# Layer-norm statistics kept as whole 128x512 tiles instead of columns per token

## The chip, the cores and the metric

One core of one Trainium2 chip runs the whole program. The metric is device time in microseconds, the median of several executions of the same program.

## The reference

Two layers of width 2048 over 512 tokens in fp32. Layer 0 mixes block-sparse attention and a gated linear recurrence, layer 1 is a gated causal convolution of 31 taps with a layer norm of its own. Each layer ends in a projection, a residual, a layer norm and a gated side input of 256 features. The change touches the three layer norms only:

```python
def _layernorm(x, g, b):
    mu = jnp.mean(xf, axis=-1, keepdims=True)
    var = jnp.mean(jnp.square(xf - mu), axis=-1, keepdims=True)
    return ((xf - mu) * lax.rsqrt(var + LN_EPS) * g + b).astype(x.dtype)
...
# inside layer 1:
    c = _layernorm(c, ln_g, ln_b)
    return (jax.nn.silu(c) * jax.nn.silu(z)) @ w_out
...
# after each layer:
        x = _layernorm(DEEPNORM_ALPHA * x + y, post_ln_g[i], post_ln_b[i])
        x = x + (p[i] @ ple_w[i]) * jax.nn.sigmoid(x @ ple_gate_w[i])
```

## The kernel before

The activations lie transposed, features on the 128 partitions and the 512 tokens on the free axis, as 16 chunks of 128x512 in `Y`. A weight matrix is cut into tiles of 128 outputs (128x2048, "w tile"), 177 in all. Each fp32 operand is split into a high and a low part in a format that TensorE takes in one pass, and a product is three such passes: high by high, high by low, low by high. So one w tile costs TensorE 48 matmuls of 128x512. Of a w tile ACT makes the high part (`w_hi`, L895) and DVE (L1288) or POOL (L432) the low part (`w_lo`). Of a normed chunk ACT makes the high part (`a_hi`, L899) and POOL the low part (`a_lo`, L400). Each engine's program is written out by hand in its own order, and semaphores join them. The results land in two banks, `G0` and `G1`, which must be emptied in turn.

After the last tile of a layer's output projection stands this, in `second_part`, twice in the program:

- TensorE runs two "side" w tiles, each 8 groups of 6 matmuls (`ple_pack`). Group c needs its G bank empty, and a bank is emptied by a copy on ACT (`ple_out`, L1091) or DVE (`side_out`, L1716). `SIDE_ON_ACT` and `SIDE_ON_DVE` say behind which chunk of the norm each copy stands in those engines' order.
- The norm's statistics go on beside it. `ln_sum` and `ln_sqs` hold, for each partition and token, the sum of the chunks and of their squares. TensorE sums each over the partitions into a column per 128 tokens, 128x4 in all (`to_tokens`). DVE and ACT work out mean, variance and one over the deviation on 128x4 columns: a square root on ACT, a reciprocal on DVE and one Newton step. The mean, then the reciprocal deviation, is spread over the partitions again: DVE multiplies the column into a diagonal matrix (L1673) and TensorE multiplies ones by it (`spread_mean` into `X[1]`, `spread_dev` into `X[2]`).
- DVE subtracts (L1701) and multiplies (L1705) chunk after chunk. ACT applies gain and bias (L1163) and makes `a_hi`, POOL makes `a_lo`. In the same DVE program stand the low parts of three w tiles, behind chunks 1, 7 and 9.
- TensorE then runs the first two gate tiles together (`gemm_pair`): the first takes chunk k as soon as its parts are there, the second runs 7 chunks behind. All later tiles of the gate need all 16 chunks.

The norm inside layer 1 uses the same helpers. There TensorE works on six more full w tiles of the layer meanwhile, with the two spreads inside the first of them, and the low parts of those w tiles are POOL's.

```python
            def to_tokens(bank, src):
                for m in range(NT):
                    last = mm(bank[:, m:m + 1], src[:, m * P:(m + 1) * P], ones[:, 0:1])
                return last
```

Of the kernel before, what the change touches and what calls it, by code (L numbers as in the profile page):

```python
# [101 lines left out]
def constants():  # L102
# [22 lines left out]
    half_summed=4, shift_done=1, shift_ready=1, sums_set=3, centred=16, c_summed=16, squared=16, sq_summed=16, mean_sum=1,  # L125
    var_sum=1, ln_step=6, var=1, ln_root=1, ln_guess=1, diag_d=1, diag_r=1, mean_spread=1, dev_spread=1, less_mean=16, normed=16)

# [27 lines left out]
def build(nc, xT, wall, w1, w2, pT, par_in, masks_in, out):  # L155
# [8 lines left out]
    with ExitStack() as ctx:  # L164
# [37 lines left out]
        eglast = sb("eglast", [P, NT])  # L202
        stat = bias[:, 0:5 * NT]
        lb = sb("lb", [P, 4, HEADS])
# [61 lines left out]
        ln_sq = [tmp[:, 0:T], tmp[:, T:2 * T]]  # L266
        ln_shift = diag_d = tmp[:, 2 * T:3 * T]
        ln_sqs = tmp[:, 3 * T:4 * T]
        UW = T + CONV_K - 1
        ln_sum = diag_r = tmp[:, 2 * UW + 2 * T:2 * UW + 3 * T]  # L270
        U = [tmp[:, n * UW:(n + 1) * UW] for n in range(2)]
        conv_sg = tmp[:, 2 * UW:2 * UW + T]

        c_shift = c_diag_d = tmp[:, 2 * UW + T:2 * UW + 2 * T]
        c_sq = [Z[:, 12 * T:13 * T], Z[:, 13 * T:14 * T]]
# [210 lines left out]
        def _(pe):  # L486
# [324 lines left out]
            prev_turns(HEADS)  # L811
            def to_tokens(bank, src):

                for m in range(NT):
                    last = mm(bank[:, m:m + 1], src[:, m * P:(m + 1) * P], ones[:, 0:1])
                return last

            def shift(sem, n):
# [4 lines left out]
            def token_mean(n):  # L823
                pe.wait_ge(*after("shift_ready", n, 1))
                pe.wait_ge(*after("c_summed", n, KC))
                to_tokens(X[0], ln_sum).then_inc(S("mean_sum"), 1)

            def token_var(n, sqs):
                pe.wait_ge(*after("sq_summed", n, KC))
                to_tokens(TB[2], sqs).then_inc(S("var_sum"), 1)  # L830

            def spread_mean(n, diag):

                pe.wait_ge(*after("diag_d", n, 1))
                mm(X[1][:, :], ones[:, :], diag).then_inc(S("mean_spread"), 1)

            def spread_dev(n):
                pe.wait_ge(*after("diag_r", n, 1))
                mm(X[2][:, :], ones[:, :], diag_r).then_inc(S("dev_spread"), 1)

            def second_part(layer, between=None):
                w, g = W_OUT[layer], G_OUT[layer]
                gemm_pair(w, g, f"act_hi{layer}", f"act_split{layer}", between, pair_lag=OUT_LAG[layer])
                gemms(w + 2, g + 2, 6)
                gemm(Idx(w + 8), Idx(g + 8))
                shift(*after("half_summed", 2 * layer, KC // 2))
# [7 lines left out]
                ple_pack(layer, 0, range(2, 3))
                spread_mean(n, diag_d)
                ple_pack(layer, 0, range(3, 4))
                spread_dev(n)
                ple_pack(layer, 0, range(4, 8))
# [17 lines left out]
            token_var(1, c_sqs)  # L876
            gemm(Idx(W_CONV + 42), Idx(G_CONV + 42), between={3: lambda: spread_mean(1, c_diag_d), 7: lambda: spread_dev(1)})
            gemms(W_CONV + 43, G_CONV + 43, 4)
# [8 lines left out]
        def _(act):  # L887
# [226 lines left out]
            def load_root_table():  # L1114

                f(stat[:, 3 * NT:4 * NT], ones[:, 0:NT], ACT.Sqrt)

            def deviation(n):

                var, dev = stat[:, 2 * NT:3 * NT], stat[:, 3 * NT:4 * NT]  # L1120
                act.wait_ge(*after("var", n, 1))
                f(dev, var, ACT.Sqrt).then_inc(S("ln_root"), 1)

            def second_part(layer):
# [157 lines left out]
        def _(dve):  # L1282
# [384 lines left out]

            def statistics(n, diag_of_mean):

                mean, off, var, dev, rr = [stat[:, k * NT:(k + 1) * NT] for k in range(5)]  # L1670

                def spread(dst, src):
                    return tt(dst.rearrange("p (c t) -> p c t", c=NT), ident.unsqueeze(1).broadcast_to([P, NT, P]),  # L1673
                              src.unsqueeze(2).broadcast_to([P, NT, P]), ALU.mult)

                step = S("ln_step")
                dve.wait_ge(*after("mean_sum", n, 1))
                ts(mean, X[0][:, 0:NT], 1.0 / D, None, ALU.mult).then_inc(step, 1)
                dve.wait_ge(*after("ln_step", n, 1))
                stt(off, mean, -1.0, mean, op0=ALU.mult, op1=ALU.mult).then_inc(step, 1)  # L1680
                dve.wait_ge(*after("ln_step", n, 2))
                ts(off, off, EPS, None, ALU.add).then_inc(step, 1)
                dve.wait_ge(*after("ln_step", n, 3))
                dve.wait_ge(*after("var_sum", n, 1))
                stt(var, TB[2][:, 0:NT], 1.0 / D, off, op0=ALU.mult, op1=ALU.add).then_inc(S("var"), 1)
                dve.wait_ge(*after("centred", n, KC))
                spread(diag_of_mean, mean).then_inc(S("diag_d"), 1)
                dve.wait_ge(*after("ln_root", n, 1))
                dve.reciprocal(dev, dev).then_inc(S("ln_guess"), 1)
                dve.wait_ge(*after("ln_guess", n, 1))  # L1690
                stt(rr, dev, -0.5, dev, op0=ALU.mult, op1=ALU.mult).then_inc(step, 1)
                dve.wait_ge(*after("ln_step", n, 4))
                dve.wait_ge(*after("var", n, 1))
                tt(rr, rr, var, ALU.mult).then_inc(step, 1)
                dve.wait_ge(*after("ln_step", n, 5))
                stt(dev, rr, 1.5, dev, op0=ALU.add, op1=ALU.mult).then_inc(step, 1)
                dve.wait_ge(*after("ln_step", n, 6))
                spread(diag_r, dev).then_inc(S("diag_r"), 1)

            def minus_mean(j):  # L1700
                tt(chunk(Y, j), chunk(Y, j), X[1][:, :], ALU.subtract).then_inc(S("less_mean"), 1)  # L1701

            def over_deviation(n, j):
                dve.wait_ge(*after("less_mean", n, j + 1))
                tt(chunk(Y, j), chunk(Y, j), X[2][:, :], ALU.mult).then_inc(S("normed"), 1)  # L1705

            def second_part(layer):
# [72 lines left out]
                add_last(n_ln, KC - 1, ln_sqs, ln_sq[1])  # L1780
                statistics(n_ln, diag_d)
                dve.wait_ge(*after("mean_spread", n_ln, 1))
                for j in range(3):
                    minus_mean(j)
                dve.wait_ge(*after("dev_spread", n_ln, 1))
                for j in range(KC):
                    over_deviation(n_ln, j)
                    if j + 3 < KC:
                        minus_mean(j + 3)
                    if j in (1, 7, 9):  # L1790
# [85 lines left out]
            add_last(1, KC - 1, c_sqs, c_sq[1])  # L1876
            statistics(1, c_diag_d)

# [6 lines left out]

            dve.wait_ge(*after("mean_spread", 1, 1))
            minus_mean(0)
            dve.wait_ge(*after("dev_spread", 1, 1))
            for j in range(KC + 4):
                if j + 1 < KC:  # L1890
                    minus_mean(j + 1)
                if j < KC:
                    over_deviation(1, j)
                if 4 <= j and j < KC + 2:
                    gate_c(j - 4)
# [82 lines left out]
```

## Time and profile before

| what | value |
|---|---|
| median of 3 runs | 2109.95 us (2109.76 to 2110.11) |
| profiled execution, its own time | 2109.43 us |
| profiled execution, span | 2107.8 us |
| busy: PE, PEld, DVE, ACT, POOL | 2100.7, 1743.7, 1253.4, 817.5, 365.1 us |
| granted TensorE clock over the run | 1.0 of full speed (2.4 GHz) |
| chain that ended last | PE 96%, DVE 1%, POOL 1%, ACT 1% |

The span is what the engines' records cover. The execution's own time has 1.6 us around it. PE is TensorE's matmuls, PEld its weight loads beside them. A matmul's record is longer than its turn on the engine (0.39 us for a step of 0.23 us), since the ends are modelled, so short waits of TensorE hide in the busy share and must be read from the distance between two starts.

### The profile page before, as it was taken

What the parts mean: (1) busy time and instruction counts of PE and PEld (TensorE: products, weight loads), DVE (VectorE), ACT (ScalarE), POOL (GpSimd) and SP (SyncE); (2) the same over time, 40 slices, a digit from 0 to 9 for tenths busy, and PEclk for the clock granted to TensorE, in tenths of its full rate; (3) what the DMA queues carried; (4) which work ended last, traced back from release to release, by engine and by line L of the source; (5) the groups of instructions that cost most, each with busy time, mean ns of one, the idle gap of its engine ahead of it and who ended that gap; (6) DMA issues with size and microseconds to landing.
All of it is one profiled execution on the core that took longest, in us unless ns stands there. A gap on an engine that the chain in (4) does not pass through costs nothing.

```text
span 2107.8 us, 28778 instructions
## 1 busy us (share of the span) xinstructions
PE 2100.7 (100%) x10540; PEld 1743.7 (83%) x10540; DVE 1253.4 (59%) x2105; ACT 817.5 (39%) x1041; POOL 365.1 (17%) x194
## 2 busy tenths in 40 slices
PE   9999999999999999999999999999999999999999
PEld 7888888888888888888788888888888888887888
DVE  5224575665755746356733588888888873467332
ACT  4224464564654657123722322222223441227221
POOL 0000000000000004000400034444757430004000
PEclk9999999999999999999999999999999999999999
DMA  8222222122122123322233322222222243222331
GB/s 317 81 100 80 81 81 80 63 77 80 63 97 80 60 80 127 129 93 100 88 122 124 135 97 86 97 100 100 100 97 86 97 169 110 87 93 80 137 113 69
DMA packets 33028, 213.63 MB, mean 101 GB/s; under 512 B 3904, under 2 KB 4176, under 8 KB 9408
## 3 DMA queue, kind: packets, MB, share of 16 engines
q1 hardware_dynamic: 28224, 189.54, 25.6%
q0 software_dynamic: 4448, 22.72, 2.7%
q8 instruction: 35, 0.57, 0.1%
q10 hardware_dynamic: 288, 0.52, 0.1%
q14 instruction: 33, 0.27, 0.0%
HBM read 204.39 MB, written 8.39 MB: 101 GB/s over the span
## 4 chain that ended last, share of the span: by engine, by line
PE 96%; DVE 1%; POOL 1%; ACT 1%; issue 0%; DMA 0%; DVEq 0%; ACTq 0%
PE G L488 89%; PE X L488 5%; PE T L488 1%; POOL a_lo L418 1%; PE T L670 1%; DMA Y<-xT_in 0%; DVE a_lo L1293 0%; DVE Y L1884 0%; ACT Z L1091 0%; PE T L791 0%; ACT Y L1163 0%; ACT a_hi L899 0%; DVE w_lo L1288 0%; PE T L796 0%; ACT w_hi L895 0%
## 5 line engine op out<-in xcount | busy, mean ns | idle before, releaser
L488 PE MATMUL G<-a_hi,w_hi 128*128 128x512 f32 (+1 forms) x2780 | 1087.3, 391 | 1.6 <-DVE w_lo L1288 0.6
L488 PE MATMUL G<-a_lo,w_hi 128*128 128x512 f32 (+1 forms) x2780 | 1078.3, 389 | 0.0
L488 PE MATMUL G<-a_hi,w_lo 128*128 128x512 f32 x2764 | 1074.3, 389 | 0.0
L895 ACT ACTIVATE w_hi<-w_raw 128x2048 fp32r<-128x2048 f32 x174 | 333.4, 1916 | 966.5 <-PE G L488 953.6
L1288 DVE TENSOR_TENSOR w_lo<-w_raw,w_hi 128x2048 fp32r<-128x2048 f32 x127 | 294.8, 2321 | 642.1 <-ACT w_hi L895 637.4
L488 PEld LDWEIGHTS G<-a_hi,w_hi 128*128 128x128 f32 x2780 | 522.4, 188 | 112.3 <-DVE w_lo L1288 2.2
L488 PEld LDWEIGHTS G<-a_lo,w_hi 128*128 128x128 f32 x2780 | 522.5, 188 | 107.2 <-issue 1.2
L488 PEld LDWEIGHTS G<-a_hi,w_lo 128*128 128x128 f32 x2764 | 519.3, 188 | 106.8 <-issue 0.2
L1859 DVE SCALAR_TENSOR_TENSOR T<-tmp,par,T 128x512 f32<-128x512 f32 x464 | 306.9, 751 | 0.0
L432 POOL TENSOR_TENSOR w_lo<-w_raw,w_hi 128x2048 fp32r<-128x2048 f32 x46 | 212.3, 4616 | 240.5 <-ACT w_hi L895 240.5
L400 POOL TENSOR_TENSOR a_lo<-Y,a_hi 128x512 fp32r<-128x512 f32 x32 | 44.2, 1403 | 368.1 <-ACT a_hi L899 367.8
L411 POOL CAST v_lo<-Y 128x512 fp32r<-128x512 f32 x1 | 0.6, 609 | 450.3 <-PE X L488 450.3
L414 POOL DMA_DIRECT2D Z<-pT_in x1 | 0.5, 530 | 331.1 <-PE X L488 331.1
L899 ACT ACTIVATE a_hi<-Y 128x512 fp32r<-128x512 f32 x80 | 46.1, 621 | 5.4 <-PE G L488 2.6
L1847 DVE TENSOR_TENSOR tmp<-G,tmp 128x512 f32<-128x512 f32 x16 | 11.0, 688 | 59.5 <-PE G L488 59.5
L1112 ACT ACTIVATE tmp<-Y 128x512 f32 (+1 forms) x32 | 19.6, 630 | 64.1 <-DVE Y L1745 58.5
L991 ACT ACTIVATE Z<-Z,nmx 128x128 f32<-128x128 f32 (+1 forms) x64 | 35.2, 552 | 20.8 <-DVE nmx L1573 20.7
L488 PE MATMUL G<-pk,w_hi 128*128 128x512 f32 x128 | 42.6, 414 | 0.5 <-ACT Z L1091 0.5
L1112 ACT ACTIVATE Z<-Y 128x512 f32 (+1 forms) x16 | 10.1, 633 | 76.0 <-POOL Y L449 72.7
L408 POOL DMA_DIRECT2D x_residual<-Y x16 | 8.7, 543 | 154.4 <-DVE Y L1800 154.4
L1701 DVE TENSOR_TENSOR Y<-Y,X 128x512 f32<-128x512 f32 x48 | 32.3, 680 | 4.7 <-PE X L488 4.4
L1884 DVE TENSOR_TENSOR Y<-Y,Z 128x512 f32<-128x512 f32 x16 | 28.2, 1768 | 10.7 <-ACT Z L1224 5.6
(262 smaller groups left out, 1639.4 us busy)
## 6 DMA issues: line engine op xcount, KB each, us to landing
w_raw<-wall_in SPq DMA_DIRECT2D x174, 1024.0 KB, 4.8
Y<-w_in POOLq DMA_DIRECT2D x2, 2048.0 KB, 16.0
Y<-xT_in POOLq DMA_DIRECT2D x4, 1024.0 KB, 8.1
x_residual<-Y POOLq DMA_DIRECT2D x16, 256.0 KB, 3.7
Y<-x_residual POOLq DMA_DIRECT2D x4, 1024.0 KB, 5.6
out<-Y POOLq DMA_DIRECT2D x15, 256.0 KB, 3.7
w_raw<-wall_in SPq DMA_DIRECT2D x12, 256.0 KB, 7.7
Z<-xT_in SPq DMA_DIRECT2D x6, 512.0 KB, 9.3
```

What stands on the lines that cost most here:

```text
L400: pool.tensor_tensor(a_lo[:, j, :], chunk(Y, j), a_hi[:, j, :].bitcast(F), ALU.subtract).then_inc(S(f"x1_split{layer}"), 1)
L418: pool.tensor_tensor(a_lo[:, c, :], chunk(Y, c), a_hi[:, c, :].bitcast(F), ALU.subtract).then_inc(S("act_split0"), 1)
L432: pool.tensor_tensor(w_lo[:, w.slot, :], w_raw[:, w.slot, :], w_hi[:, w.slot, :].bitcast(F), ALU.subtract).then_inc(S("w_split"), 1)
L488: return pe.matmul(o, l, r, start=start, stop=stop)
L895: f(w_hi[:, w.slot, :], w_raw[:, w.slot, :], ACT.Copy).then_inc(S("w_hi"), 1)
L899: f(a_hi[:, j, :], chunk(Y, j), ACT.Copy).then_inc(S(sem), 1)
L991: f(prob_of(ti), prob_of(ti), ACT.Exp, bias=nmx[:, o + ti:o + ti + 1], accum_out=rsum[:, o + ti:o + ti + 1]).then_inc(S("exps"), 1)
L1112: f(dst, chunk(Y, c), ACT.Square).then_inc(S("squared"), 1)
L1288: tt(w_lo[:, w.slot, :], w_raw[:, w.slot, :], w_hi[:, w.slot, :].bitcast(F), ALU.subtract).then_inc(S("w_split"), 1)
L1701: tt(chunk(Y, j), chunk(Y, j), X[1][:, :], ALU.subtract).then_inc(S("less_mean"), 1)
L1859: stt(acc, src, cw, acc, op0=ALU.mult, op1=ALU.add).then_inc(S("tap"), 1)
L1884: tt(chunk(Y, j), chunk(Y, j), chunk(Z, j), ALU.mult).then_inc(S("gated"), 1)
```

## The change

The two sums over partitions are taken with ones as the stationary operand and the sum tile as the moving one, so that every partition gets every token's sum, 128x512, in `X[0]` and `TB[2]`. Mean, variance and reciprocal deviation are worked out on 128x512 tiles. ACT squares the mean (`squared_mean`), the mean is subtracted straight from `X[0]` with the factor inside the instruction, and the reciprocal deviation is made in place in `X[2]`. Both diagonals, both spreads and the four-column operations are gone. The subtractions now run two chunks ahead of the multiplications instead of three (one in the convolution's norm).

```diff
             def token_mean(n):
                 pe.wait_ge(*after("shift_ready", n, 1))
                 pe.wait_ge(*after("c_summed", n, KC))
-                to_tokens(X[0], ln_sum).then_inc(S("mean_sum"), 1)
+                mm(X[0][:, :], ones[:, :], ln_sum).then_inc(S("mean_sum"), 1)
 
             def token_var(n, sqs):
                 pe.wait_ge(*after("sq_summed", n, KC))
-                to_tokens(TB[2], sqs).then_inc(S("var_sum"), 1)
-
-            def spread_mean(n, diag):
-
-                pe.wait_ge(*after("diag_d", n, 1))
-                mm(X[1][:, :], ones[:, :], diag).then_inc(S("mean_spread"), 1)
-
-            def spread_dev(n):
-                pe.wait_ge(*after("diag_r", n, 1))
-                mm(X[2][:, :], ones[:, :], diag_r).then_inc(S("dev_spread"), 1)
+                mm(TB[2][:, :], ones[:, :], sqs).then_inc(S("var_sum"), 1)
...
-            gemm(Idx(W_CONV + 42), Idx(G_CONV + 42), between={3: lambda: spread_mean(1, c_diag_d), 7: lambda: spread_dev(1)})
+            gemm(Idx(W_CONV + 42), Idx(G_CONV + 42))
...
+            def squared_mean(n):
+
+                act.wait_ge(*after("mean_sum", n, 1))
+                f(part, X[0][:, :], ACT.Square, scale=1.0 / D).then_inc(S("ln_step"), 1)
 
             def deviation(n):
 
-                var, dev = stat[:, 2 * NT:3 * NT], stat[:, 3 * NT:4 * NT]
                 act.wait_ge(*after("var", n, 1))
-                f(dev, var, ACT.Sqrt).then_inc(S("ln_root"), 1)
+                f(X[2][:, :], var, ACT.Sqrt).then_inc(S("ln_root"), 1)
...
                 square(n_ln, KC - 1, ln_sq[1], KC - 2)
+                squared_mean(n_ln)
                 ple_out(layer, 0, 0)
                 ple_out(layer, 0, 1)
                 deviation(n_ln)
...
+            def minus_mean(j):
+                stt(chunk(Y, j), X[0][:, :], -1.0 / D, chunk(Y, j), op0=ALU.mult, op1=ALU.add).then_inc(S("less_mean"), 1)
...
+            def statistics(n):
+
+                dev, step = X[2][:, :], S("ln_step")
+                dve.wait_ge(*after("centred", n, KC))
                 dve.wait_ge(*after("ln_step", n, 1))
+                ts(part, part, -1.0, EPS, ALU.mult, ALU.add).then_inc(step, 1)
+                minus_mean(0)
...
-                stt(var, TB[2][:, 0:NT], 1.0 / D, off, op0=ALU.mult, op1=ALU.add).then_inc(S("var"), 1)
+                stt(var, TB[2][:, :], 1.0 / D, part, op0=ALU.mult, op1=ALU.add).then_inc(S("var"), 1)
+                minus_mean(1)
                 dve.wait_ge(*after("ln_root", n, 1))
                 dve.reciprocal(dev, dev).then_inc(S("ln_guess"), 1)
                 dve.wait_ge(*after("ln_guess", n, 1))
+                tt(part, var, dev, ALU.mult).then_inc(step, 1)
+                dve.wait_ge(*after("ln_step", n, 3))
+                stt(part, part, -0.5, dev, op0=ALU.mult, op1=ALU.mult).then_inc(step, 1)
                 dve.wait_ge(*after("ln_step", n, 4))
+                stt(dev, part, 1.5, dev, op0=ALU.add, op1=ALU.mult).then_inc(S("dev_ready"), 1)
+                dve.wait_ge(*after("dev_ready", n, 1))
...
-                dve.wait_ge(*after("mean_spread", n_ln, 1))
-                for j in range(3):
-                    minus_mean(j)
-                dve.wait_ge(*after("dev_spread", n_ln, 1))
                 for j in range(KC):
                     over_deviation(n_ln, j)
-                    if j + 3 < KC:
-                        minus_mean(j + 3)
+                    if j + 2 < KC:
+                        minus_mean(j + 2)
```

On TensorE, in the first side tile of layer 0, behind its group 1, stand before the change the two sums as columns (`X`, `T` from the ones and the sums in `tmp`), the side groups (`G` from the split side input `pk` and the w tile, two rows x 2 = one group) and the two spreads:

```order
L488 MATMUL X<-ones_r,tmp 128x1 x4
L488 MATMUL T<-ones_r,tmp 128x1 x4
L488 MATMUL G<-pk,w_hi 128x512 x2
L488 MATMUL G<-pk,w_lo 128x512
L488 MATMUL G<-pk,w_hi 128x512 x2
L488 MATMUL G<-pk,w_lo 128x512
L488 MATMUL X<-tmp,ones_r 128x512
L488 MATMUL G<-pk,w_hi 128x512 x2
L488 MATMUL G<-pk,w_lo 128x512
L488 MATMUL G<-pk,w_hi 128x512 x2
L488 MATMUL G<-pk,w_lo 128x512
L488 MATMUL X<-tmp,ones_r 128x512
```

The same place on TensorE after the change:

```order
L488 MATMUL X<-tmp,ones_r 128x512
L488 MATMUL T<-tmp,ones_r 128x512
L488 MATMUL G<-pk,w_hi 128x512 x2
L488 MATMUL G<-pk,w_lo 128x512
L488 MATMUL G<-pk,w_hi 128x512 x2
L488 MATMUL G<-pk,w_lo 128x512
L488 MATMUL G<-pk,w_hi 128x512 x2
L488 MATMUL G<-pk,w_lo 128x512
```

Eight one-column matmuls became two whole ones, and the two whole ones further on are gone, so nothing of the norm stands between the side groups any more.

On DVE, at the same place in layer 0, the statistics before the change (`bias` is the buffer in which the columns lie), up to the low part of the w tile behind chunk 1, with what each row waits for:

```order
L1685 SCALAR_TENSOR_TENSOR bias<-T,bias 128x4 [waits var_sum,ln_step]
L1673 TENSOR_TENSOR tmp<-par,bias 128x512 [waits centred]
L1689 RECIPROCAL bias<-bias 128x4 [waits ln_root]
L1691 SCALAR_TENSOR_TENSOR bias<-bias 128x4 [waits ln_guess]
L1694 TENSOR_TENSOR bias<-bias 128x4 [waits var,ln_step]
L1696 SCALAR_TENSOR_TENSOR bias<-bias 128x4 [waits ln_step]
L1673 TENSOR_TENSOR tmp<-par,bias 128x512 [waits ln_step]
L1701 TENSOR_TENSOR Y<-Y,X 128x512 [waits mean_spread]
L1701 TENSOR_TENSOR Y<-Y,X 128x512 x2
L1705 TENSOR_TENSOR Y<-Y,X 128x512 [waits less_mean,dev_spread]
```

And after the change, up to that low part:

```order
L1667 TENSOR_SCALAR tmp<-tmp 128x512 [waits ln_step,centred]
L1656 SCALAR_TENSOR_TENSOR Y<-X,Y 128x512
L1671 SCALAR_TENSOR_TENSOR tmp<-T,tmp 128x512 [waits var_sum,ln_step]
L1656 SCALAR_TENSOR_TENSOR Y<-X,Y 128x512
L1674 RECIPROCAL X<-X 128x512 [waits ln_root]
L1676 TENSOR_TENSOR tmp<-tmp,X 128x512 [waits ln_guess]
L1678 SCALAR_TENSOR_TENSOR tmp<-tmp,X 128x512 [waits ln_step]
L1680 SCALAR_TENSOR_TENSOR X<-tmp,X 128x512 [waits ln_step]
L1660 TENSOR_TENSOR Y<-Y,X 128x512 [waits less_mean,dev_ready]
L1656 SCALAR_TENSOR_TENSOR Y<-X,Y 128x512
L1660 TENSOR_TENSOR Y<-Y,X 128x512 [waits less_mean]
L1275 TENSOR_TENSOR w_lo<-w_raw,w_hi 128x2048 [waits w_hi]
```

Every operation of the statistics has 512 elements in place of 4, the reciprocal among them. Two subtractions stand among them instead of three behind them.

## Rows read from the trace of the kernel before

**Rows 1.** The page: busy time by engine, and TensorE's granted clock in 40 slices.
```profile
PE 2100.7 (100%) x10540; PEld 1743.7 (83%) x10540; DVE 1253.4 (59%) x2105; ACT 817.5 (39%) x1041; POOL 365.1 (17%) x194
...
PEclk9999999999999999999999999999999999999999
```

**Rows 2.** Timeline of PE, first post-norm: start, duration (us), instruction [idle before, releaser].
```profile
1001.19 0.95 PE L488 MATMUL X<-ones_r,tmp 128*128 128x1 f32 x8
...
1002.90 0.71 PE L488 MATMUL G<-pk,w_hi 128*128 128x512 f32 x2
...
1003.68 0.64 PE L488 MATMUL G<-pk,w_hi 128*128 128x512 f32 x2
...
1004.39 1.02 PE L488 MATMUL X<-tmp,ones_r 128*128 128x512 f32 x2
...
1005.94 0.62 PE L488 MATMUL G<-pk,w_hi 128*128 128x512 f32 x2
...
1013.54 0.71 PE L488 MATMUL G<-pk,w_hi 128*128 128x512 f32 x2 [0.27 <-ACT Z L1091]
```

**Rows 3.** Instruction groups of DVE by form: busy us, mean ns | idle before.
```profile
L1447 DVE RECIPROCAL rg<-rg 128x8 f32<-128x8 f32 x8 | 1.6, 203 | 28.6 <-ACT tmp L1039 28.6
L1447 DVE RECIPROCAL rg<-rg 128x4 f32<-128x4 f32 x8 | 1.4, 172 | 0.0
...
L1583 DVE TENSOR_SCALAR nmx<-nmx 128x4 f32<-128x4 f32 x8 | 1.4, 170 | 0.3
...
L1589 DVE TENSOR_SCALAR tmp<-tmp 128x512 f32<-128x512 f32 x8 | 3.4, 428 | 0.3
...
L1701 DVE TENSOR_TENSOR Y<-Y,X 128x512 f32<-128x512 f32 x48 | 32.3, 680 | 4.7 <-PE X L488 4.4
```

**Rows 4.** Timeline of DVE over the first post-norm.
```profile
1007.69 0.69 DVE L1705 TENSOR_TENSOR Y<-Y,X 128x512 f32<-128x512 f32 x1 [0.36 <-PE X L488]
...
1010.09 2.29 DVE L1288 TENSOR_TENSOR w_lo<-w_raw,w_hi 128x2048 fp32r<-128x2048 f32 x1
1012.29 0.68 DVE L1705 TENSOR_TENSOR Y<-Y,X 128x512 f32<-128x512 f32 x1
...
1015.21 0.69 DVE L1716 COPY Z<-G 128x512 f32<-128x512 f32 x1 [0.45 <-PE G L488]
...
1021.80 3.40 DVE L1288 TENSOR_TENSOR w_lo<-w_raw,w_hi 128x2048 fp32r<-128x2048 f32 x1
```

**Rows 5.** Timeline of ACT over the first post-norm.
```profile
1009.59 0.81 ACT L1163 ACTIVATE Y<-Y,par 128x512 f32<-128x512 f32 x1
1010.43 0.63 ACT L899 ACTIVATE a_hi<-Y 128x512 fp32r<-128x512 f32 x1
...
1013.80 0.81 ACT L1163 ACTIVATE Y<-Y,par 128x512 f32<-128x512 f32 x1
...
1022.45 0.60 ACT L1091 ACTIVATE Z<-G 128x512 f32<-128x512 f32 x1 [0.29 <-PE G L488]
...
1031.03 0.82 ACT L1163 ACTIVATE Y<-Y,par 128x512 f32<-128x512 f32 x1 [0.55 <-DVE Y L1705]
```

**Rows 6.** Timeline of POOL over the first post-norm.
```profile
1019.00 4.05 POOL L400 TENSOR_TENSOR a_lo<-Y,a_hi 128x512 fp32r<-128x512 f32 x3 [2.36 <-ACT a_hi L899]
...
1033.71 7.56 POOL L400 TENSOR_TENSOR a_lo<-Y,a_hi 128x512 fp32r<-128x512 f32 x6
```

**Rows 7.** Timeline of PE at the end of the first gate tile.
```profile
1041.18 0.64 PE L488 MATMUL G<-a_lo,w_hi 128*128 128x512 f32 x2
```

**Rows 8.** Timeline at the convolution's norm: POOL, DVE, ACT, DVE.
```profile
1661.73 4.58 POOL L432 TENSOR_TENSOR w_lo<-w_raw,w_hi 128x2048 fp32r<-128x2048 f32 x1 [8.26 <-ACT w_hi L895]
...
1666.72 0.69 DVE L1701 TENSOR_TENSOR Y<-Y,X 128x512 f32<-128x512 f32 x1 [2.91 <-PE X L488]
...
1672.24 1.92 ACT L895 ACTIVATE w_hi<-w_raw 128x2048 fp32r<-128x2048 f32 x1 [8.67 <-PE G L488]
...
1675.37 4.03 DVE L1884 TENSOR_TENSOR Y<-Y,Z 128x512 f32<-128x512 f32 x1 [2.58 <-ACT Y L1267]
```

More of the change, by code:

```diff
@@ L125 @@
     half_summed=4, shift_done=1, shift_ready=1, sums_set=3, centred=16, c_summed=16, squared=16, sq_summed=16, mean_sum=1,
-    var_sum=1, ln_step=6, var=1, ln_root=1, ln_guess=1, diag_d=1, diag_r=1, mean_spread=1, dev_spread=1, less_mean=16, normed=16)
+    var_sum=1, ln_step=4, var=1, ln_root=1, ln_guess=1, dev_ready=1, less_mean=16, normed=16)
 class Idx:
@@ L202, in build @@
         eglast = sb("eglast", [P, NT])
-        stat = bias[:, 0:5 * NT]
         lb = sb("lb", [P, 4, HEADS])
@@ L266, in build @@
         ln_sq = [tmp[:, 0:T], tmp[:, T:2 * T]]
-        ln_shift = diag_d = tmp[:, 2 * T:3 * T]
+        ln_shift = tmp[:, 2 * T:3 * T]
         ln_sqs = tmp[:, 3 * T:4 * T]
+        part, var = ln_sq
         UW = T + CONV_K - 1
-        ln_sum = diag_r = tmp[:, 2 * UW + 2 * T:2 * UW + 3 * T]
+        ln_sum = tmp[:, 2 * UW + 2 * T:2 * UW + 3 * T]
         U = [tmp[:, n * UW:(n + 1) * UW] for n in range(2)]
         conv_sg = tmp[:, 2 * UW:2 * UW + T]
-        c_shift = c_diag_d = tmp[:, 2 * UW + T:2 * UW + 2 * T]
+        c_shift = tmp[:, 2 * UW + T:2 * UW + 2 * T]
         c_sq = [Z[:, 12 * T:13 * T], Z[:, 13 * T:14 * T]]
@@ L811, in _ @@
             prev_turns(HEADS)
[L812 to L816, printed above, removed]
             def shift(sem, n):
@@ L853, in second_part @@
                 token_var(n, ln_sqs)
[L854 to L858, printed above, removed]
+                ple_pack(layer, 0, range(2, 8))
                 ple_pack(layer, 1)
@@ L1114, in load_root_table @@
             def load_root_table():
-                f(stat[:, 3 * NT:4 * NT], ones[:, 0:NT], ACT.Sqrt)
+                f(bias[:, 0:NT], ones[:, 0:NT], ACT.Sqrt)
+            def squared_mean(n):
+                act.wait_ge(*after("mean_sum", n, 1))
+                f(part, X[0][:, :], ACT.Square, scale=1.0 / D).then_inc(S("ln_step"), 1)
             def deviation(n):
-                var, dev = stat[:, 2 * NT:3 * NT], stat[:, 3 * NT:4 * NT]
                 act.wait_ge(*after("var", n, 1))
-                f(dev, var, ACT.Sqrt).then_inc(S("ln_root"), 1)
+                f(X[2][:, :], var, ACT.Sqrt).then_inc(S("ln_root"), 1)
             def second_part(layer):
@@ L1256, in _ @@
             square(1, KC - 1, c_sq[1], None)
+            squared_mean(1)
             deviation(1)
@@ L1666, in add_last, with over_deviation @@
                 tt(sqs, sqs, sq, ALU.add).then_inc(S("sq_summed"), 1)
[L1668 to L1678, printed above, removed]
+            def minus_mean(j):
+                stt(chunk(Y, j), X[0][:, :], -1.0 / D, chunk(Y, j), op0=ALU.mult, op1=ALU.add).then_inc(S("less_mean"), 1)
+            def over_deviation(n, j):
+                dve.wait_ge(*after("less_mean", n, j + 1))
+                tt(chunk(Y, j), chunk(Y, j), X[2][:, :], ALU.mult).then_inc(S("normed"), 1)
+            def statistics(n):
+                dev, step = X[2][:, :], S("ln_step")
+                dve.wait_ge(*after("centred", n, KC))
                 dve.wait_ge(*after("ln_step", n, 1))
-                stt(off, mean, -1.0, mean, op0=ALU.mult, op1=ALU.mult).then_inc(step, 1)
+                ts(part, part, -1.0, EPS, ALU.mult, ALU.add).then_inc(step, 1)
+                minus_mean(0)
                 dve.wait_ge(*after("ln_step", n, 2))
-                ts(off, off, EPS, None, ALU.add).then_inc(step, 1)
-                dve.wait_ge(*after("ln_step", n, 3))
                 dve.wait_ge(*after("var_sum", n, 1))
-                stt(var, TB[2][:, 0:NT], 1.0 / D, off, op0=ALU.mult, op1=ALU.add).then_inc(S("var"), 1)
-                dve.wait_ge(*after("centred", n, KC))
-                spread(diag_of_mean, mean).then_inc(S("diag_d"), 1)
+                stt(var, TB[2][:, :], 1.0 / D, part, op0=ALU.mult, op1=ALU.add).then_inc(S("var"), 1)
+                minus_mean(1)
                 dve.wait_ge(*after("ln_root", n, 1))
@@ L1690, in statistics @@
                 dve.wait_ge(*after("ln_guess", n, 1))
-                stt(rr, dev, -0.5, dev, op0=ALU.mult, op1=ALU.mult).then_inc(step, 1)
+                tt(part, var, dev, ALU.mult).then_inc(step, 1)
+                dve.wait_ge(*after("ln_step", n, 3))
+                stt(part, part, -0.5, dev, op0=ALU.mult, op1=ALU.mult).then_inc(step, 1)
                 dve.wait_ge(*after("ln_step", n, 4))
[L1693 to L1705, printed above, removed]
+                stt(dev, part, 1.5, dev, op0=ALU.add, op1=ALU.mult).then_inc(S("dev_ready"), 1)
+                dve.wait_ge(*after("dev_ready", n, 1))
             def second_part(layer):
@@ L1780, in second_part @@
                 add_last(n_ln, KC - 1, ln_sqs, ln_sq[1])
-                statistics(n_ln, diag_d)
-                dve.wait_ge(*after("mean_spread", n_ln, 1))
-                for j in range(3):
-                    minus_mean(j)
-                dve.wait_ge(*after("dev_spread", n_ln, 1))
+                statistics(n_ln)
                 for j in range(KC):
                     over_deviation(n_ln, j)
-                    if j + 3 < KC:
-                        minus_mean(j + 3)
+                    if j + 2 < KC:
+                        minus_mean(j + 2)
                     if j in (1, 7, 9):
@@ L1876, in _ @@
             add_last(1, KC - 1, c_sqs, c_sq[1])
-            statistics(1, c_diag_d)
+            statistics(1)
             def gate_c(j):
@@ L1884, in gate_c @@
                 tt(chunk(Y, j), chunk(Y, j), chunk(Z, j), ALU.mult).then_inc(S("gated"), 1)
-            dve.wait_ge(*after("mean_spread", 1, 1))
-            minus_mean(0)
-            dve.wait_ge(*after("dev_spread", 1, 1))
             for j in range(KC + 4):
-                if j + 1 < KC:
-                    minus_mean(j + 1)
                 if j < KC:
                     over_deviation(1, j)
+                if j + 2 < KC:
+                    minus_mean(j + 2)
                 if 4 <= j and j < KC + 2:
```

## The prediction

> **What bounds the kernel now.** I read the page first. TensorE is busy for practically the whole span and its granted clock is full in all forty slices [rows 1]. So time that leaves TensorE's own program is gained, if nothing makes TensorE wait in its place, and any new wait of TensorE is lost. Then I read TensorE's timeline at the three norms by the distance between starts, as durations overlap. Half a side group takes 0.71 us (1003.68 to 1004.39) [rows 2]. After the first side tile one start is held up until a copy of ACT has emptied the bank [rows 2]. The timelines of DVE, ACT and POOL show how close this is. At 1015.21 DVE waits 0.45 us for TensorE and at 1022.45 ACT waits 0.29 us for it, but at 1031.03 ACT waits 0.55 us for a DVE multiplication [rows 4, 5]. From 1033.71 POOL makes six low parts without a break and ends at 1041.27 [rows 6]. The last matmul of the first gate tile needs the last of these and starts at about 1041.43, 0.25 us behind the one before (0.64 less 0.39) against 0.23 elsewhere [rows 7]. So TensorE gets there with nothing to spare: in the post-norms TensorE and the chain DVE, ACT, POOL run neck and neck. What the statistics take on DVE counts there in full.
>
> **TensorE.** The two column sums take from 1001.19 to 1002.90, 1.71 us. A whole 128x512 product of ones costs 1005.94 less 1004.39, 1.55, less the half group's 0.71: 0.84 us, and its result is there 1.02 us after its start [rows 2]. Before there were 1.71 + 2 x 0.84 = 3.39 us per norm, after 1.68. TensorE's program gets 1.7 us shorter at each of three norms.
>
> **The statistics of a post-norm.** I follow the first. The mean's product starts at 1001.19 as before and is ready at 1002.2. A result is taken about 0.03 us after its maker ends (1009.59 + 0.81, then 1010.43) [rows 5].
> - ACT squares the mean out of PSUM: 0.60 us as the copy of this size [rows 5], to 1002.85.
> - DVE negates it and adds epsilon: between 0.43 us (the one-input form) and 0.68 us (two inputs) [rows 3]. I take 0.43, to 1003.3. Then one subtraction, whose issue slot is 0.60 us (four operations from 1007.69 to 1010.09) [rows 4], to 1003.9, and the variance, 0.69, to 1004.6.
> - ACT's square root, 0.60, to 1005.2. The second subtraction lies beside it and costs nothing while the root takes as long.
> - The reciprocal of 512 columns, in place. No row has it. Below lies 0.68 us, the price of any whole-tile operation. Above stands what its own rows give: 4 elements 172 ns, 8 elements 203 ns, so 7.75 ns for each more [rows 3], and for 508 more 3.94 us, 4.11 us in all. An ordinary operation has 170 ns at 4 elements and 680 at 512, 1.0 ns each [rows 3], so the steep slope belongs to the reciprocal. I take 4.11, to 1009.3.
> - Three Newton operations, each waiting for the one before: 3 x 0.72, to 1011.55.
>
> The first multiplication then starts at 1011.6 instead of 1007.69 [rows 4]: 3.9 us later.
>
> The Trainium skill (VectorE: DVE Perf Modes, First, the fixed hardware budget) says that the reciprocal runs an iterative divide with a repeat count of 8 where simple operations run once; by that, an estimate of eight times 1.0 ns an element, it would take 4.3 us and the sum below would be 0.4 us larger. The slope in the trace agrees.
>
> **What the later start does.** Behind chunk 1 DVE makes a low part of a w tile. Before, it began at 1010.09, 2.40 us after the first multiplication [rows 4]. POOL begins its first low part when ACT has done gain and bias and `a_hi`: 0.69 + 0.84 + 0.63 and some 0.1 for the handing over, 2.27 us after that multiplication. Before, ACT came to it later, at 1009.59, being busy with a copy, and DVE was first. POOL and DVE exclude each other there: POOL's third piece of three ended at 1023.05 and DVE's low part, issued at 1021.80, took 3.40 us where it takes 2.29 alone [rows 4, 6]. Now ACT waits for DVE, so POOL wins by 0.13 us, holds DVE for the rest of its 1.26 us piece, and DVE's next multiplication moves from 1012.29 to 1017.3, 5.0 us later. The Trainium skill (SBUF — State Buffer, Who interferes with whom) has the same lock, held for the whole instruction; the 3.40 us row agrees.
>
> The 0.45 us that DVE waited at 1015.21 for a side group is used up: 4.6 us. From there nothing gives way. TensorE waits for DVE's copies of the side groups, ACT's copy at 1022.45 waits for TensorE, the high part of a w tile stands behind it on ACT, its low part and the later multiplications behind that on DVE, then ACT, POOL, and TensorE's last matmul of the first gate tile [rows 5 to 7]. The subtractions' shorter lead (two instead of three) adds 0.6 us of DVE work, which goes into DVE's waits. TensorE's own 1.7 us are gained first and then waited away: it must stand about 3.9 us before group 7 of the first side tile, whose bank is emptied by the ACT copy that stands behind chunk 0, and nearly 2 us before the second side tile. So each post-norm makes the end **4.6 us later**, net; two make 9.2. All that comes after is led by TensorE and moves along.
>
> **The convolution's norm.** DVE stood idle 2.91 us before 1666.72, waiting for a spread that TensorE reached late, and again 2.58 us before 1675.37 [rows 8]. By the steps above the multiplications start near 1667.9 instead of 1667.3, and the second idle stretch takes that up. ACT now squares and roots ahead of the high part of the next w tile, so POOL's low part begins near 1663.3 instead of 1661.73 and ends near 1667.9. TensorE wants it when the present tile ends, before at about 1672.2, now 1670.5 [rows 8]: 2.6 us to spare. If that cover were gone, each microsecond would cost one. So here the 1.7 us stay gained.
>
> **Sum.** 2 x 4.6 - 1.7 = +7.5 us. The profiled execution took 2109.43, which gives 2116.9; the median of the runs is 0.5 above it, so 2117.4.
>
> **The rivals.**
> - *The lost race.* If DVE's low part starts before POOL's piece, DVE keeps 1.1 us: 3.5 each, 2 x 3.5 - 1.7 = +5.3, 2115.2. The margin is only 0.13 us, but each term in it is read from rows.
> - *A cheap reciprocal.* If it streams like any tile at 0.68 us, the first multiplication is 0.5 us later, the lock adds 1.1, and DVE's idle time takes some 0.4: 1.2 each, +0.7, 2110.6, no change. For: no row has more than 8 elements. Against: the two sizes, on 8 instructions each. At 2 us it would be +3.3, still no change.
> - *Faster.* The mechanism is TensorE alone: 3 x 1.7 = -5.1, 2104.8, if the chain beside it is not what ends last. The page speaks for it (TensorE 100% busy, DVE 59%) [rows 1]. Against it: as the two run neck and neck, a post-norm gives its 1.7 us only where the first multiplication comes 1.7 us earlier too, 4.8 us behind the mean's product instead of 6.5, and the new steps take 6.3 us without the reciprocal. Over 0.2% faster begins where they take 5.2.
> - *TensorE's clock falls.* TensorE would stand still for 3.9 us and soon again for 2. The trace has the full 2.4 GHz level throughout and no wait of this length [rows 1]. If it were granted 1.2 GHz for 7 to 10 us behind the stall, steps would double; the side groups wait anyway, so 1.1 to 2.7 us more each remain: +9.7 to +12.9, about 2121. The Trainium skill (TensorE: Matmul & The Clock Gate, What's actually happening) says that an idle array is throttled until it is busy again; no row here shows it.
>
> **How the numbers follow.** This kernel's runs tell 0.2% (4.2 us) from no change. Forecast as summed, between 2115.5 and 2119.5: 0.68. Lost race: 0.08. Cheap reciprocal: 0.12. Faster: 0.04. Clock: 0.08. Faster 0.04, same 0.12, slower 0.84. The range leaves out the cheap reciprocal at its lowest, the faster case and the worst of the clock: from 2112.5 (a reciprocal of 3 us with the race lost gives +3.1) to 2120.5.
>
> **What would show it.** In the changed kernel's profile: RECIPROCAL on 128x512 at 4.0 to 4.4 us; two ones products at 0.84 us spacing where the columns were; a TensorE wait of 3.5 to 4 us before group 7 of both first side tiles, ended by an ACT copy; a low part of DVE held by POOL behind chunk 1; the first gate tile ending 4.6 us late; nothing waiting in the convolution's norm. A reciprocal below 2 us, or a post-norm whose side tiles have no wait, would make the prediction wrong.

## The result and the profile after

The changed kernel takes 2116.64 us in the median against 2109.86 us, 1.0034 times the time before (95% interval 1.002 to 1.0049): slower by 0.3%. A few executions, of either kernel and of some experiments, were some 7 us slower and are in the ratios (without them this one is 1.003), while two others, at 3005 and 7560 us, are left out. The profiled execution has a span of 2115.2 us against 2107.8.

First TensorE's waits over the whole run, from the view of waits: us in total, times, longest. The first line is TensorE's matmuls into a G bank waiting for an ACT copy of that bank into `Z`, the second the same matmuls waiting for the low part of a w tile.

```profile
PE G L488 <- ACT Z L1072: 6.4, 4, 2.9
...
PE G L488 <- DVE w_lo L1275: 1.4, 2, 0.9
```

Before, no wait behind an ACT copy was longer than the one in [rows 2]. Now there are two of 2.9 us, one in each post-norm. To see what each norm gained or lost I read TensorE's timeline at marks that both programs have: the start of the norm's first sum, and the start of the third gate tile (the matmul behind the pair). Before (PE timeline, start and duration in us):

```profile
1047.32 0.39 PE L488 MATMUL G<-a_hi,w_hi 128*128 128x512 f32 x1
...
1657.49 0.95 PE L488 MATMUL X<-ones_r,tmp 128*128 128x1 f32 x8
...
1905.00 0.95 PE L488 MATMUL X<-ones_r,tmp 128*128 128x1 f32 x8
...
1951.16 0.39 PE L488 MATMUL G<-a_hi,w_hi 128*128 128x512 f32 x1
```

And after:

```profile
1001.08 1.02 PE L488 MATMUL X<-tmp,ones_r 128*128 128x512 f32 x2
...
1051.55 0.39 PE L488 MATMUL G<-a_hi,w_hi 128*128 128x512 f32 x1
...
1661.72 1.02 PE L488 MATMUL X<-tmp,ones_r 128*128 128x512 f32 x2
...
1907.39 1.02 PE L488 MATMUL X<-tmp,ones_r 128*128 128x512 f32 x2
...
1958.58 0.39 PE L488 MATMUL G<-a_hi,w_hi 128*128 128x512 f32 x1
```

From the first sum (before at 1001.19, [rows 2]) to the third gate tile a post-norm took 46.13 and 46.16 us, and now takes 50.47 and 51.19: 4.34 and 5.03 more. From the convolution's first sum to the second post-norm's it took 247.51 and now takes 245.67: 1.84 less. The work between the first post-norm and the convolution's norm takes 610.17 us in both. 4.34 + 5.03 - 1.84 - 0.11 (by which the first sum came earlier) = 7.4, the whole difference of the spans.

DVE's timeline of the first post-norm after the change, against [rows 4]:

```profile
1005.13 3.37 DVE L1674 RECIPROCAL X<-X 128x512 f32<-128x512 f32 x1
...
1010.70 0.69 DVE L1660 TENSOR_TENSOR Y<-Y,X 128x512 f32<-128x512 f32 x1
...
1013.10 3.30 DVE L1275 TENSOR_TENSOR w_lo<-w_raw,w_hi 128x2048 fp32r<-128x2048 f32 x1
1016.32 0.68 DVE L1660 TENSOR_TENSOR Y<-Y,X 128x512 f32<-128x512 f32 x1
...
1019.42 0.69 DVE L1692 COPY Z<-G 128x512 f32<-128x512 f32 x1 [0.62 <-PE G L488]
```

POOL's in the same place:

```profile
1012.98 1.27 POOL L400 TENSOR_TENSOR a_lo<-Y,a_hi 128x512 fp32r<-128x512 f32 x1 [175.09 <-ACT a_hi L880]
...
1036.65 8.81 POOL L400 TENSOR_TENSOR a_lo<-Y,a_hi 128x512 fp32r<-128x512 f32 x7 [0.59 <-ACT a_hi L880]
```

The group of the three reciprocals (busy us, mean ns):

```profile
L1674 DVE RECIPROCAL X<-X 128x512 f32<-128x512 f32 x3 | 10.1, 3367 | 0.2
```

The reciprocal on 512 columns takes 3.37 us. The first multiplication starts at 1010.70, 3.0 us later than in [rows 4]. POOL's first low part (1012.98) is 0.12 us ahead of DVE's (1013.10), which takes 3.30 us instead of 2.29. The next multiplication is 4.0 us late. POOL ends its last piece at 1045.46, where it ended at 1041.27 [rows 6].

At 1019.42 DVE waits for TensorE, though its own copy comes 4.2 us later than before. That wait was not foreseen. TensorE's timeline shows why:

```profile
1013.44 1.22 PE L488 MATMUL G<-pk,w_hi 128*128 128x512 f32 x2 [2.87 <-ACT Z L1072]
1014.46 0.63 PE L488 MATMUL G<-pk,w_lo 128*128 128x512 f32 x1
1014.88 1.05 PE L488 MATMUL G<-pk,w_hi 128*128 128x512 f32 x2
...
1019.85 0.39 PE L488 MATMUL G<-pk,w_lo 128*128 128x512 f32 x1
```

The two matmuls at 1014.88 take 0.86 us to the next start, where two take 0.46 at full clock. The stretches of both post-norms, by windows (busy us and instructions by engine, then the granted clock, DMA share, GB/s):

```profile
1006.00:1013.40 7.40, 4.56 (x20) 3.35 (x18) 7.26 (x9) 3.14 (x6) 0.42 (x1) 0.96 0.00 0
1013.40:1019.20 5.80, 5.67 (x13) 3.98 (x14) 5.39 (x5) 4.53 (x7) 4.18 (x3) 0.50 0.24 72
...
1912.00:1920.90 8.90, 6.02 (x26) 4.50 (x25) 8.76 (x9) 4.29 (x7) 1.28 (x1) 0.99 0.00 0
1920.90:1927.40 6.50, 5.62 (x14) 3.93 (x13) 5.88 (x8) 4.50 (x6) 4.01 (x2) 0.50 0.45 161
```

Around the end of each wait TensorE was granted half its clock, 1.2 GHz, and by narrower windows it had it for 6.8 us each time. In the first post-norm the fall came 0.6 us before the wait ended (the 0.96 of the first row), in the second about 1.0 us after it (the wait ended at 1919.76).

At the convolution's norm nothing waits on TensorE, as forecast. DVE and POOL there, against [rows 8]:

```profile
1667.67 4.62 POOL L432 TENSOR_TENSOR w_lo<-w_raw,w_hi 128x2048 fp32r<-128x2048 f32 x1 [9.97 <-ACT w_hi L876]
...
1671.36 0.69 DVE L1660 TENSOR_TENSOR Y<-Y,X 128x512 f32<-128x512 f32 x1
...
1677.77 4.03 DVE L1856 TENSOR_TENSOR Y<-Y,Z 128x512 f32<-128x512 f32 x1 [0.34 <-ACT Y L1254]
```

DVE's idle time ahead of the first gating product shrank from 2.58 to 0.34 us, and the product is held by POOL for as long as before.

### The profile page after: what moved, and what is told of

Its sections match the earlier page's. It is cut to its first block, busy times and chain, and to the rows that moved or that the text cites. A ratio compares the mean times of both kernels' runs of the same rounds, so it can differ in the third digit from the quotient of the medians.

```text
span 2115.2 us, 28674 instructions
## 1 busy us (share of the span) xinstructions
PE 2101.4 (99%) x10492; PEld 1740.5 (82%) x10492; DVE 1266.6 (60%) x2093; ACT 821.2 (39%) x1044; POOL 365.7 (17%) x194
## 4 chain that ended last, share of the span: by engine, by line
PE 96%; DVE 2%; POOL 1%; issue 0%; DMA 0%; ACT 0%; DVEq 0%; ACTq 0%
PE G L488 88%; PE X L488 5%; PE T L488 1%; POOL a_lo L418 1%; PE T L670 1%; DVE w_lo L1275 0%; DMA Y<-xT_in 0%; DVE X L1674 0%; DVE a_lo L1280 0%; DVE Y L1856 0%; DVE Y L1656 0%; PE T L791 0%; DVE Y L1660 0%; PE T L796 0%; ACT w_hi L876 0%
## 5 line engine op out<-in xcount | busy, mean ns | idle before, releaser
L488 PEld LDWEIGHTS G<-pk,w_hi 128*128 128x128 f32 x128 | 25.8, 207 | 17.5 <-ACT Z L1072 8.9
```

Source lines behind the costliest of these rows:

```text
L488: return pe.matmul(o, l, r, start=start, stop=stop)
```

## The experiments

All are read by the same stretches: a post-norm from its first sum to the third gate tile, and the convolution's from its first sum to the second post-norm's.

| kernel | first post-norm | second | convolution | span | median us |
|---|---|---|---|---|---|
| before | 46.13 | 46.16 | 247.51 | 2107.8 | 2109.4 |
| the change | 50.47 | 51.19 | 245.67 | 2115.2 | 2116.6 |
| filler matmuls | 49.79 | 49.79 | 245.66 | 2113.4 | 2115.2 |
| copy first | 50.58 | 51.37 | 245.71 | 2116.0 | 2117.6 |
| reciprocal on 4 columns | 46.67 | 46.66 | 245.67 | 2108.4 | 2108.9 |
| convolution only | 46.17 | 46.12 | 245.68 | 2105.9 | 2107.7 |
| one over the root on ACT | 45.37 | 45.36 | 245.70 | 2104.6 | 2106.1 |
| fillers, POOL waits | 49.02 | 49.01 | 245.67 | 2111.4 | 2113.3 |
| second reciprocal, convolution | 49.79 | 49.77 | 245.70 | 2114.3 | 2116.1 |
| no Newton step | 45.00 | 44.96 | 245.71 | 2103.8 | 2105.5 |

**Filler matmuls** in TensorE's waits:

```diff
+            def fill(times):
+
+                for _ in range(times):
+                    mm(X[1][:, :], ones_r[:, :], p_hi[:, 0, :])
...
-                ple_pack(layer, 0, range(2, 8))
+                ple_pack(layer, 0, range(2, 7))
+                fill(12)
+                ple_pack(layer, 0, range(7, 8))
+                fill(6)
                 ple_pack(layer, 1)
```

> The change, with 12 extra one-pass 128x512 matmuls into the idle bank X[1] ahead of side group 7 and 6 more ahead of the second side tile, in both post-norms; nothing reads them. They fill TensorE's waits there (2.87 us and about 1.5 us) without outlasting them. Measure: the post-norm stretch on TensorE, from the start of the mean's product to the start of the third gate tile, 46.13 and 46.16 us before, 50.47 and 51.19 with the change. Theory (chain plus clock): in the change the clock fell to half for some 6 us behind the wait, and the side groups run then made DVE wait 0.62 us once in the first post-norm and twice in the second. With TensorE kept busy the clock stays at 2.4 GHz, and the stretches become about 49.8 and 49.9, 1.9 us less in all. Rival (the clock costs nothing, as the groups wait anyway): 50.5 and 51.2, no change in time. Rival (idleness of this length does not set the clock): granted clock still below 1.0 behind the same place.

Measured: 2115.17 us, 1.0023 (1.0012 to 1.0033) of before, stretches 49.79 and 49.79. The same windows as above:

```profile
1013.40:1019.20 5.80, 5.65 (x23) 4.17 (x23) 5.80 (x7) 4.43 (x8) 4.20 (x3) 1.00 0.18 45
...
1920.90:1927.40 6.50, 6.50 (x28) 4.65 (x27) 6.50 (x10) 5.16 (x7) 3.92 (x2) 1.00 0.50 161
```

With TensorE kept busy the clock stays full, DVE's wait at the side group's copy is gone (its busy time fills both windows), and the two stretches become equal, 0.68 and 1.40 us shorter. Adding work to the bound engine made these stretches shorter. So the fall of the clock cost 2.1 us in the change's profiled execution, and the rival that it costs nothing has fallen for that execution. By the medians, each against before's of its own series, it is 6.8 less 5.7, 1.1 us, and the two ratios' intervals overlap. The changed kernel's own executions point the same way: those with a mean granted clock of 0.997 and a span below 2120 us had spans of 2115.2 and 2115.3, those with 0.998 2114.3 and 2114.8, those with 0.999 2113.8 and 2114.1.

**Copy first**: the copy that ends the 2.9 us wait, moved ahead of what it waited for.

```diff
-SIDE_ON_ACT = {0: ((0, 5),), 1: ((0, 6), (0, 7)), ...
+SIDE_ON_ACT = {1: ((0, 6), (0, 7)), ...
...
-                for c in range(2, 5):
+                for c in range(2, 6):
                     ple_out(layer, 0, c)
```

> The change, with ACT's copy of side group 5 ahead of chunk 0 of the norm instead of behind it, in both post-norms. Rival (TensorE's wait of 2.87 us for that copy is itself what the change lost): the wait goes and each stretch gets 2.9 us shorter, 47.6 and 48.3. Theory (the chain DVE, ACT, POOL sets the end; the wait is only where TensorE's lead is given back): the wait moves behind group 7, to the second side tile, and is longer there (some 4.9 us); the end of the stretch does not come earlier. With the clock's fall behind the wait now lying on side groups that DVE and ACT wait for, it comes later, by up to 1.4 us: 50.5 to 51.9.

Measured: 2117.64 us, 1.0039 (1.0025 to 1.0054), stretches 50.58 and 51.37, not shorter but 0.1 and 0.2 us longer. TensorE's timeline shows the wait moved to the second side tile:

```profile
1016.90 0.97 PE L488 MATMUL G<-pk,w_hi 128*128 128x512 f32 x2 [4.48 <-DVE w_lo L1275]
...
1923.38 1.22 PE L488 MATMUL G<-pk,w_hi 128*128 128x512 f32 x2 [4.48 <-DVE w_lo L1275]
```

TensorE's longest wait is thus the place where its lead is given back, not the loss. Taking it away there gains nothing, since DVE's chain sets the end. The clock fell here too: in the first post-norm just after the wait, for 3.4 us, and in the second 1.6 us before the wait ended, for 6.8 us.

**Reciprocal on 4 columns** (it leaves out the other 508):

```diff
-                dve.reciprocal(dev, dev).then_inc(S("ln_guess"), 1)
+                dve.reciprocal(dev[:, 0:NT], dev[:, 0:NT]).then_inc(S("ln_guess"), 1)
```

> The change, with the reciprocal on 4 of its 512 columns in all three norms: it leaves out 508 columns of the reciprocal. So it prices the whole-tile reciprocal. Theory (the reciprocal's 3.37 us pass to the end one to one, and the clock's fall with them, as TensorE then hardly waits): the first multiplication 3.2 us earlier, post-norm stretches about 46.8 each, 0.7 over those of before because of the lock between POOL and DVE behind chunk 1; whole time 2109.5, within 0.1% of before. Rival (the other whole-tile operations and the subtractions' shorter lead carry the loss): stretches above 49.

Measured: 2108.94 us, 0.9996 (0.9987 to 1.0006), stretches 46.67 and 46.66. Against the fillers' 49.79, where the clock is full as well, that is 3.12 us a post-norm for 3.2 us less on DVE: one to one. The 0.5 us by which a post-norm still lies over before's is not the price of the other whole-tile operations alone, for POOL wins the race behind chunk 1 here too (DVE's timeline):

```profile
1011.50 3.35 DVE L1275 TENSOR_TENSOR w_lo<-w_raw,w_hi 128x2048 fp32r<-128x2048 f32 x1
```

That lock costs 0.8 us by the run in which POOL waits, further down. So the other whole-tile operations cost no more than TensorE's shorter program gives back.

**Convolution only**: the change in the convolution's norm, the post-norms as before.

```diff
             def token_mean(n):
...
+                if n == 1:
+                    mm(X[0][:, :], ones[:, :], ln_sum).then_inc(S("mean_sum"), 1)
+                    return
                 to_tokens(X[0], ln_sum).then_inc(S("mean_sum"), 1)
...
-            statistics(1, c_diag_d)
+            statistics_c(1)
```

> The kernel before, with the change made in the convolution's norm alone; both post-norms as before. Theory (there TensorE's 1.7 us are gained in full, since DVE's idle time takes the reciprocal): from the start of the convolution's mean to that of the second post-norm 245.7 us instead of 247.51, post-norm stretches 46.1, whole time about 2108.1. Rival (the gain there comes from the post-norm ahead of it, or is spent again): no change, 2109.9.

Measured: 2107.69 us, 0.9992 (0.9982 to 1.0001). The interval alone does not tell this from no change. In the trace the convolution's stretch is 245.68 and the post-norms are as before, so the 1.8 us are this norm's own.

**One over the root on ACT**, with the Newton step kept:

```diff
...
-                f(X[2][:, :], var, ACT.Sqrt).then_inc(S("ln_root"), 1)
+                f(X[2][:, :], var, ACT.Abs_reciprocal_sqrt).then_inc(S("ln_root"), 1)
...
-                dve.reciprocal(dev, dev).then_inc(S("ln_guess"), 1)
-                dve.wait_ge(*after("ln_guess", n, 1))
```

> The change, with ACT making one over the root itself (Abs_reciprocal_sqrt in place of Sqrt, its table loaded where the root's was) and DVE's reciprocal gone; the Newton step stays, so the computation is whole. Theory (reciprocal, lock and clock are all that the change lost): the first multiplication falls to about its old distance from the mean's product, TensorE no longer waits 2.9 us, so the clock stays up; post-norm stretches about 45.5 (0.7 under before) if DVE's low part wins against POOL behind chunk 1, 46.6 if POOL wins; with the convolution's 1.8 us the whole time is 2106.3 to 2108.5, below both kernels. Rival (whole-tile statistics are too long even so): stretches above 47 and time not below 2109.4.

Measured: 2106.14 us, 0.9988 (0.9979 to 0.9997), 3.3 us by the medians: below both kernels. DVE's timeline:

```profile
1006.88 0.70 DVE L1678 SCALAR_TENSOR_TENSOR X<-tmp,X 128x512 f32<-128x512 f32 x1
1007.61 0.69 DVE L1660 TENSOR_TENSOR Y<-Y,X 128x512 f32<-128x512 f32 x1
...
1010.01 2.28 DVE L1275 TENSOR_TENSOR w_lo<-w_raw,w_hi 128x2048 fp32r<-128x2048 f32 x1
```

The first multiplication is back at 6.2 us behind the first sum (1001.38), DVE wins against POOL (2.28 us; POOL's first low part starts at 1010.15, 0.14 us behind), and the post-norms are 0.8 us under before.

**Fillers, POOL waits**: the race behind chunk 1 given to DVE, on top of the fillers.

```diff
             def x1_low(layer):

+                pool.wait_ge(S("w_split"), Idx(W_OUT[layer] + 17).n(1))
```

> The change with the filler matmuls (clock kept up), and POOL's first low part of each post-norm waiting until DVE's low part of the w tile behind chunk 1 is done, so that DVE wins there. Theory (the lock costs DVE 1.1 us there and nothing later takes that up): stretches 48.7 instead of 49.8. Rival (the later waits for TensorE and ACT take it up): 49.8, unchanged.

Measured: 2113.29 us, 1.0019 (1.0009 to 1.0028), stretches 49.02 and 49.01, 0.8 us shorter than with the fillers alone instead of 1.1. DVE's timeline:

```profile
1013.01 2.28 DVE L1284 TENSOR_TENSOR w_lo<-w_raw,w_hi 128x2048 fp32r<-128x2048 f32 x1
...
1017.85 0.69 DVE L1701 COPY Z<-G 128x512 f32<-128x512 f32 x1 [0.16 <-PE G L489]
```

The low part gets its 1.0 us back, and 0.16 us of it go into a wait for TensorE. The lock costs 0.8 us a post-norm.

**Second reciprocal in the convolution's norm**:

```diff
+                if n == 1:
+                    dve.reciprocal(X[1][:, :], dev)
                 dve.reciprocal(dev, dev).then_inc(S("ln_guess"), 1)
```

> The change with a second reciprocal of 128x512 in the convolution's norm alone (its result goes to the idle X[1]): 3.4 us more on DVE ahead of the first multiplication. Theory (DVE is idle or held by POOL's low part there until 1681.3, so the reciprocal is covered): from the start of the convolution's mean to that of the second post-norm's 245.7 us, unchanged. Rival (DVE is just in time there as in the post-norms): 249.

Measured: 2116.06 us, 1.0032 (1.002 to 1.0044), the convolution's stretch 245.70, unchanged. DVE's timeline:

```profile
1669.53 3.30 DVE L1676 RECIPROCAL X<-X 128x512 f32<-128x512 f32 x1
...
1675.04 0.69 DVE L1660 TENSOR_TENSOR Y<-Y,X 128x512 f32<-128x512 f32 x1
...
1681.03 1.25 DVE L1858 TENSOR_TENSOR Y<-Y,Z 128x512 f32<-128x512 f32 x1
```

The gating product comes later (1681.03) but is held for 1.25 us in all instead of 4.03, and ends where it would have. So the reciprocal is hidden there twice over. Its post-norms are those of the change, with the same two waits of 2.87 us, and yet came out at 49.79 and 49.77. Its windows behind these waits:

```profile
1014.60:1020.50 5.90, 5.81 (x18) 4.05 (x18) 5.90 (x7) 4.63 (x7) 4.28 (x3) 0.73 0.29 86
...
1921.00:1928.00 7.00, 5.64 (x23) 3.93 (x23) 7.00 (x10) 5.67 (x8) 4.10 (x3) 1.00 0.41 150
```

In the second the clock did not fall at all, and in the first it fell for 3.4 us, half as long as in the change's profiled execution. Both stretches are those of the fillers. So nothing but the clock is seen to differ with the fillers, and the clock's price differs between executions: nothing here, 0.68 and 1.40 us in the change's profiled one. The span here is 0.9 us above the fillers' although all three stretches agree: the first sum starts 0.8 us later (1002.23 against 1001.40). A start of this kind is in every span and median, so the stretches tell small differences more safely.

**No Newton step** (it leaves out the three sharpening operations), with one over the root on ACT and POOL waiting:

```diff
...
-                tt(part, var, dev, ALU.mult).then_inc(step, 1)
-                dve.wait_ge(*after("ln_step", n, 3))
-                stt(part, part, -0.5, dev, op0=ALU.mult, op1=ALU.mult).then_inc(step, 1)
-                dve.wait_ge(*after("ln_step", n, 4))
-                stt(dev, part, 1.5, dev, op0=ALU.add, op1=ALU.mult).then_inc(S("dev_ready"), 1)
-                dve.wait_ge(*after("dev_ready", n, 1))
```

> As the version with ACT making one over the root, but without the Newton step: it leaves out the three operations that sharpen the root, 2.2 us on DVE; and POOL's first low part waits for DVE's. Theory (in the post-norms DVE's chain sets the end down to where TensorE's own 1.7 us per norm are earned, and copies and low parts behind that): stretches 44.5 to 45.0, whole time about 2105. Rival (TensorE already led at 45.5): unchanged at 45.5.

Measured: 2105.47 us; the ratio, 0.9992 (0.9982 to 1.0002), is less clear than the medians (0.998). Stretches 45.00 and 44.96: 2.2 us less on DVE give only 0.4, and DVE now waits for TensorE:

```profile
1014.24 0.69 DVE L1685 COPY Z<-G 128x512 f32<-128x512 f32 x1 [1.72 <-PE G L489]
```

Here one to one ends: DVE arrives early and waits for the side group. The stretches are 1.1 and 1.2 us under before, not the 1.84 that TensorE's shorter program gave in the convolution's norm. What takes the remaining 0.7 us is not shown.

## Why the prediction was right

Its time, 2117.4 us, and the measured 2116.6 are 0.8 us apart. The mechanism is shown, but that the number came so close is in part luck. Three steps held. TensorE's own saving of 1.7 us a norm is there in full where DVE has cover (1.84 in the convolution's norm, also alone and with a doubled reciprocal). The post-norms go by DVE's chain: 3.2 us less of it gave 3.1 us, and taking away TensorE's own wait gave nothing. And POOL wins the race behind chunk 1, by 0.12 us where 0.13 was forecast, for 0.8 us at the end where 1.1 was reckoned.

Two terms were off and largely made up for each other. With the clock kept up (the fillers) a post-norm lost 3.7 and 3.6 us where 4.6 was forecast, and the stretches add up to 5.4 us, not 7.5.

- The reciprocal was priced at 4.11 us by the slope between 4 and 8 elements [rows 3]. It takes 3.37, or 6.3 ns for each further element instead of 7.75 ((3367 - 170) / 508). That is 0.74 us too much in each post-norm, 1.5 in all. By the repeat count of 8 in the Trainium skill (VectorE: DVE Perf Modes, First, the fixed hardware budget) the prediction's estimate was 4.3; the measurement decides.
- That the clock would stay up was taken as the likely case and its fall given 0.08. It fell in both post-norms and cost 0.68 and 1.40 us, 2.1 in all, by the fillers (about 1.1 in the medians). The reason given, that the trace of before had no wait of this length, was no sign that the clock would stay up. For the case of a fall the prediction took 7 to 10 us at 1.2 GHz, for which it had no row, and 1.1 to 2.7 us lost in each post-norm. Measured were 6.8 us each and the 0.68 and 1.40 us above, the first below that range and the second inside it. The trace shows where the loss enters: DVE waits for a slowed side group before its copies, once in the first post-norm (0.62 us) and twice in the second (0.62 and 0.61).

The sum by its steps at measured sizes: 2 x (4.6 - 0.74) + 2.1 - 1.84 = 8.0, against 7.4 in the spans; the lock's smaller price, 0.3 in each post-norm, is about the rest. The wait of TensorE before group 7 was 2.9 us where 3.5 to 4 were named as the sign, for the cheaper reciprocal.

The cheap reciprocal, the rival with the highest chance, was wrong in its price, but its consequence was borne out by the run on 4 columns: 2108.9, no change. The faster rival, TensorE's program alone, would have needed a post-norm's statistics within 5.2 us. At 6.2 us, with one over the root on ACT, the kernel is 0.12% faster. At 4.1 us, without the Newton step, DVE no longer leads, and even there the medians are 4.0 us apart, less than the 5.1 of that rival.

## What to carry to other kernels

Where the saturated engine and a chain beside it arrive together, count the chain, not the busy shares: here 3.2 us more on an engine that is busy 60% of the time cost 3.1 us each. Before a few-column operation is turned into a whole tile, price its slowest member by its cost per element; the same change was a gain in the norm where DVE had idle time. And read a long new wait of TensorE twice, for what ends it and for what clock TensorE has behind it.

## What the runs showed of the hardware

- DVE's reciprocal has a price per element of its own: 172 ns on 4 elements and 203 on 8 [rows 3], 3367 on 512, where a product of two tiles takes 0.68 us on 512.
- One and the same wait of TensorE, 2.87 us in the same code of the post-norms, went with 6.8 us at 1.2 GHz twice in one execution, and with 3.4 us and none in an execution of another kernel (the second reciprocal). With the copy first it was a wait of 4.48 us in both post-norms, once with a granted clock of 1.00 up to its end and 0.72 over the 6.0 us behind it, and once with the fall 1.6 us before its end and 6.8 us at the lower level. So the length of the wait does not settle whether the clock falls, when, or for how long. What does stays open, and part of the spread of the changed kernel's runs may come from it. The Trainium skill (TensorE: Matmul & The Clock Gate, What's actually happening) has the two levels and that idleness leads to the lower one; the windows at 0.50 agree.
- Matmuls that nobody reads, put into such a wait, kept the clock at 2.4 GHz in both post-norms, which were 2.1 us shorter in all than in the change's profiled execution.
- ACT's table function for one over the root takes the place of root and reciprocal at the root's price, 0.60 us on 128x512 for either: the first multiplication followed 6.2 us behind the first sum instead of 9.6.
